# A diffusion layer on one Trainium2 core: sixteen modulation units move from the mixer into the first feed-forward block

## The reference

```python
m_x = split(silu(c) @ w_ada + b_ada, 9)          # 9 vectors of 1024
m_c = split(silu(c_ctx) @ w_ada + b_ada, 9)
x   = x   + 0.5 * m_x[2] * swiglu(modulate(rmsnorm(x, g0), m_x[0], m_x[1]), ffn1)
ctx = ctx + 0.5 * m_c[2] * swiglu(modulate(rmsnorm(ctx, g0), m_c[0], m_c[1]), ffn1)
px = modulate(rmsnorm(x, g1), m_x[3], m_x[4]) @ w_in
pc = modulate(rmsnorm(ctx, g1), m_c[3], m_c[4]) @ w_in
y  = concat(retention(px, pc), gmlp(px))
x  = x + m_x[5] * (y @ w_out)
x  = x + 0.5 * m_x[8] * swiglu(modulate(rmsnorm(x, g2), m_x[6], m_x[7]), ffn2)
return rmsnorm(x, final_g)
```

## Time and profile before

| what | value |
|---|---|
| timed runs, median (lowest to highest) | 2081.57 us (2080.06 to 2083.95) |
| the profiled execution, and its span | 2077.21 us, 2075.4 us |
| PE busy | 2018.5 us, 97% of the span |
| DVE, ACT, POOL busy | 1267.8, 753.2, 495.3 us |
| granted TensorE clock, mean over the span | 0.989 |
| chain of work that ended last | PE 85%, DVE 9%, ACT 3% |

### The profile page before, as it was taken

The page is one execution under the profiler, slowest core; times in us unless marked ns, Lnnn a source line. Parts: engine busy times, 40 slices in busy tenths (PEclk is TensorE's granted clock), DMA queues, the critical chain, the costliest instruction groups (busy, mean ns, idle before and its releaser), DMA issues.

```text
span 2075.4 us, 26060 instructions
## 1 busy us (share of the span) xinstructions
PE 2018.5 (97%) x10112; PEld 1690.5 (81%) x10112; DVE 1267.8 (61%) x1883; ACT 753.2 (36%) x1093; POOL 495.3 (24%) x311
## 2 busy tenths in 40 slices
PE   8999999999999999999999999898999999999997
PEld 4999978888888887887988898676788888888886
DVE  4987765556555466575353458889565555455555
ACT  3233533333333354463212222246333333344342
POOL 1000033323211102023323223455323322210002
PEclk9999999999999999999999999999999999999998
DMA  7874426656444776641010333421566644466664
GB/s 307 344 273 145 153 78 219 200 192 231 161 130 160 242 234 177 212 145 62 21 41 21 115 119 122 142 102 56 176 204 209 215 155 167 148 209 194 193 193 153
DMA packets 104042, 343.52 MB, mean 166 GB/s; under 512 B 11760, under 2 KB 13040, under 8 KB 86896
## 3 DMA queue, kind: packets, MB, share of 16 engines
q1 hardware_dynamic: 99312, 325.08, 46.3%
q10 hardware_dynamic: 4608, 16.78, 2.5%
HBM read 267.36 MB, written 74.45 MB: 165 GB/s over the span
## 4 chain that ended last, share of the span: by engine, by line
PE 85%; DVE 9%; ACT 3%; issue 2%; DMA 1%; POOL 1%; SPq 0%; ACTq 0%; DVEq 0%; POOLq 0%
PE PS L2111 13%; PE PS L2113 13%; PE PS L2112 12%; PE PS L1966 7%; PE PS L1968 6%; PE PS L1967 6%; PE PS L2151 6%; PE PS L2153 6%; PE PS L2152 6%; PE PS L2069 4%; DVE AS L1431 2%; PE PS L2024 1%; PE PS L2324 1%; DVE WVL L1551 1%; DVE DG L1323 1%
## 5 line engine op out<-in xcount | busy, mean ns | idle before, releaser
L2111 PE MATMUL PS<-HH,WVH 128*128 128x512 f32 x672 | 265.1, 395 | 0.0
L2113 PE MATMUL PS<-HH,WVL 128*128 128x512 f32 x672 | 263.7, 392 | 0.0
L2112 PE MATMUL PS<-HL,WVH 128*128 128x512 f32 x672 | 262.0, 390 | 0.0
L1966 PE MATMUL PS<-HH,WH 128*128 128x512 f32 x416 | 168.5, 405 | 3.2 <-DVE WL L1727 3.2
L1551 DVE TENSOR_TENSOR WVL<-WR,WVH 128x512 fp32r<-128x512 f32 x160 | 115.1, 719 | 88.2 <-ACT WVH L989 88.1
L1967 PE MATMUL PS<-HL,WH 128*128 128x512 f32 x416 | 164.4, 395 | 0.0
L1968 PE MATMUL PS<-HH,WL 128*128 128x512 f32 x416 | 164.3, 395 | 0.0
L1594 DVE TENSOR_TENSOR HL<-HLF,HH 128x1024 fp32r<-128x1024 f32 x76 | 104.8, 1386 | 80.5 <-ACT HH L1037 80.4
L2113 PEld LDWEIGHTS PS<-HH,WVL 128*128 128x128 f32 x672 | 126.1, 188 | 30.0
L2112 PEld LDWEIGHTS PS<-HL,WVH 128*128 128x128 f32 x672 | 126.1, 188 | 28.2
L2111 PEld LDWEIGHTS PS<-HH,WVH 128*128 128x128 f32 x672 | 126.4, 188 | 26.8
(11 more groups left out here) (262 smaller groups left out, 4843.1 us busy)
## 6 DMA issues: line engine op xcount, KB each, us to landing
WR<-w_units SPq DMA_DIRECT2D x89, 1024.0 KB, 5.8
gated<-HB SPq DMA_DIRECT2D x44, 512.0 KB, 6.7
down_weight_sums<-WB SPq DMA_DIRECT2D x22, 1024.0 KB, 3.9
gated_sums<-TBF SPq DMA_DIRECT2D x22, 768.0 KB, 4.2
AW<-w_units ACTq DMA_DIRECT2D x32, 512.0 KB, 4.3
HLF<-down_weight_sums SPq DMA_DIRECT2D x46, 256.0 KB, 3.3
AW<-ada_units SPq DMA_DIRECT2D x11, 1024.0 KB, 13.7
W2RB<-w_units SPq DMA_DIRECT2D x22, 512.0 KB, 3.6
```

The costliest lines, as they stand in the source:

```text
L1966: pe.matmul(dst, wh, xh, start=first, stop=False)
L2111: pe.matmul(bank[:, :], wh, xh, start=first, stop=False, skip_group_check=True)
L2112: pe.matmul(bank[:, :], wh, xl, start=False, stop=False, skip_group_check=True)
L2113: ins = pe.matmul(bank[:, :], wl, xh, start=False, stop=k == 3, skip_group_check=True)
```

## The change

Three things change.

- The latents' units leave the mixer. Units 20 to 27 are worked in the periods g = 14 to 21 of the first block: DVE sums the first half of a unit ahead of `up_first`, the second half behind it; PE makes the columns behind product 4. Units 28 to 35 are worked in the down product of the first block, half a unit behind `ring_low` of step 10, 13, 18, 21, 26, ... 69; PE makes their sixteen columns together behind step 72, and DVE adds their biases before the mixer's norm work begins. The loads are one DMA of 1 MB each on SyncE's queue; ACT issues none.
- In the openings of both blocks `gate_second(1, 1)` stands behind the first sum and the first low part of the next weights, no longer behind all of them.
- Two of the first eight units (6 and 7 in the order of loading) are split like the other operands: ACT makes the high part, DVE the low part, PE multiplies 16 times in fp32r instead of 8 times in float32, with a stationary of four columns for the high part. Product 5 goes ahead of `norm_scale` on PE. The first unit's load is one DMA and no longer two halves. The exponentials of the decay go from the start into the context's periods 2 and 3.

```diff
+ADA_SPLIT = (6, 7)
-ADA_SLOTS = ((10, 5), (11, 0), (11, 2), (12, 0), (12, 2), (13, 0), (13, 3), (14, 3), (14, 7), (15, 1), (15, 4), (15, 7),
-             (16, 1), (17, 1), (18, 1), (19, 1))
+ADA_PERIODS = {14 + i: ADA_CTX + i for i in range(8)}
+ADA_STEPS = tuple(range(ADA_CTX + 8, N_ADA))
 
...
+        AWL = {n: at(f"AWL{n}", [P, KT, UC], F32R, 65728 + 8192 * (n % 4)) for n in ADA_SPLIT}
+        CSS = at("CSS", [P, KT, 4], F32R, R + 40960)
+        SEL = at("SEL", [4, 2], F32, R + 41216)
...
+        def latent_places(a):
+
+            if a in ADA_STEPS:
+                i = a - ADA_STEPS[0]
+                return HLF[:, :, UC * (i % 2):UC * (i % 2 + 1)], HHF[:, i, 0:UC], PS[1]
+            return AWB[:, :, :], ASB[:, a % 2, :], PS[5]
...
-            for half in range(2):
-                k = slice(4 * half, 4 * half + 4)
-                sp.dma_start(AW[0][:, k, :], ada_units[0][:, k, :]).then_inc(s_half if half == 0 else s_first[0], 16)
+            ada(0)
...
+                def latent_unit(a):
+                    if a in ADA_STEPS[:2]:
+                        sp.wait_ge(s_m[1], NF)
+                    elif a in ADA_STEPS:
+                        sp.wait_ge(s_adv, sums_count(a - 2))
+                    elif a == ADA_CTX:
+                        sp.wait_ge(s_w2st, 16 * HALF)
+                    else:
+                        sp.wait_ge(s_adv, sums_count(a - 1))
+                    sp.dma_start(latent_places(a)[0], ada_source(a)).then_inc(s_first[a % 2], 16)
...
+                    if f == 0 and g + 1 in ADA_PERIODS:
+                        latent_unit(ADA_PERIODS[g + 1])
...
+                    if f == 0 and s % 8 == 6 and s // 8 < len(ADA_STEPS):
+                        latent_unit(ADA_STEPS[s // 8])
...
+            for n in ADA_SPLIT:
+                act.wait_ge(s_first[n], 16)
+                act.activation(split_high(n), AW[n][:, :, :], ACT.Copy).then_inc(s_awh, 1)
...
-            def latent_unit(u):
-
-                for half in range(2):
-                    k = slice(4 * half, 4 * half + 4)
-                    if u == ADA_CTX:
-                        act.wait_ge(s_fill, FILL["yscale", HEADS - 1, 1] + 1)
-                    else:
-                        act.wait_ge(s_adv, sums_count(u - 1) - 1 + half)
-                    act.dma_start(AW2[:, k, :], ada_source(u)[:, k, :]).then_inc(s_first[half], 16)
-
...
+            def split_low(n):
+
+                dve.wait_ge(s_awh, ADA_SPLIT.index(n) + 1)
+                dve.tensor_tensor(AWL[n][:, :, :], AW[n][:, :, :], split_high(n).bitcast(F32), ALU.subtract).then_inc(s_awl, 1)
...
-            def latent_sums(a):
+            def latent_sums(a, half):
 
 
                 sums, links = sums_count(a - 1), 15 * sums_count(ADA_CTX - 1) + 6 * (a - ADA_CTX)
-                acc = AS2[a % 2]
-                if a > ADA_CTX + 1:
-                    dve.wait_ge(s_col, a - 1)
-                for k in range(KT):
-                    if k % 4 == 0:
-                        dve.wait_ge(s_first[k // 4], 16 * (a - ADA_CTX + 4))
-                    w, c = AW2[:, k, :], CS[:, k, 0:1]
+                unit, acc, _ = latent_places(a)
+                if half == 0:
+                    dve.wait_ge(s_first[a % 2], latent_load_count(a))
+                    if a in ADA_STEPS:
+                        dve.wait_ge(BS[0].m[1], NF)
+                    elif a > ADA_CTX + 1:
+                        dve.wait_ge(s_col, a - 1)
+                for k in range(4 * half, 4 * half + 4):
+                    w, c = unit[:, k, :], CS[:, k, 0:1]
                     if k == 0:
-                        ins = dve.tensor_scalar(acc[:, :], w, c, None, ALU.mult)
+                        ins = dve.tensor_scalar(acc, w, c, None, ALU.mult)
                     else:
                         if k == 4:
                             dve.wait_ge(s_adv, sums + 1)
                         else:
                             dve.wait_ge(s_asum, links + k - k // 4)
-                        ins = dve.scalar_tensor_tensor(acc[:, :], w, c, acc[:, :], ALU.mult, ALU.add)
+                        ins = dve.scalar_tensor_tensor(acc, w, c, acc, ALU.mult, ALU.add)
                     ins.then_inc(s_adv if k % 4 == 3 else s_asum, 1)
 
             dve.wait_ge(s_const, 16 * 6)
                 dve.wait_ge(s_hi, b + 1)
...
-            dve.wait_ge(s_exp, 1)
-            dve.tensor_scalar(LG[:, :], LG[:, :], -1.0, None, ALU.mult).then_inc(s_lg, 1)
             ada_rows(4)
             ada_mods(2)
+            split_low(6)
+            ada_rows(5)
             dve.wait_ge(s_rb, J[0, 0] + 1)
-            for k in range(KT):
+            for k in range(4):
                 scaled(0, 0, k)
             ada_mods(3)
             first_gain(1)
-            ada_rows(5)
+            split_low(7)
+            for k in range(4, KT):
+                scaled(0, 0, k)
+            ada_rows(6)
             ada_mods(4)
-            ada_rows(6)
             ada_mods(5)
             first_gain(2)
             block_low(0)
...
-                def next_weights(g):
+                def next_weights(g, between=lambda n: None):
                     dve.wait_ge(s_wl, weights_done(f, g - 1, ORDER1[-1] if f and g == 2 else 6))
                     dve.wait_ge(s_wraw, 16 * g)
-                    weight_sums(g, lambda n: weight_low(g, n))
+                    def low_and_more(n):
+                        weight_low(g, n)
+                        between(n)
+                    weight_sums(g, low_and_more)
                     weight_low(g, 2)
                     weight_low(g, 3)
...
                 def block_period(g, q):
+                    a = ADA_PERIODS.get(g) if f == 0 else None
                     weight_low(g, 5)
                     gated(g - 1, 1 - q, 0)
+                    if a is not None:
+                        latent_sums(a, 0)
                     up_first(g, q)
+                    if a is not None:
+                        latent_sums(a, 1)
                     if g + 1 < NF:
                         next_weights(g + 1)
                     gate_second(g, q)
                         weight_low(g + 1, 4)
                     else:
                         ring_low(0)
+                    if a is not None:
+                        latent_mods(a)
                     up_second(g, q)
                     gated(g, q, 1)
                     if g + 1 < NF:
                     token_low(2, k)
                 up_first(1, 1)
...
                 up_first(1, 1)
                 dve.wait_ge(s_wl, weights_done(f, 1, 5))
-                next_weights(2)
-                gate_second(1, 1)
+                next_weights(2, lambda n: gate_second(1, 1) if n == 0 else None)
                 weight_low(2, 4)
                 up_second(1, 1)
...
                 if s % HALF == 3 and s > HALF:
                     down_added(0, s // HALF - 1)
+                if s >= 10 and (s - 10) // 8 < len(ADA_STEPS) and s % 8 in (2, 5):
+                    latent_sums(ADA_STEPS[(s - 10) // 8], s % 8 == 5)
                 if s == 22:
                     add_squares(1, 0)
...
+            dve.wait_ge(s_col, N_ADA)
+            for a in ADA_STEPS:
+                latent_mods(a)
...
+            def split_product(n):
+                r, i = ADA_PE.index(n), ADA_SPLIT.index(n)
+                pe.wait_ge(s_awh, i + 1)
+                pe.wait_ge(s_mods, ADA_PE[r - 4] + 1)
+                for k in range(KT):
+                    pe.matmul(PS[r % 4][0:4, 0:UC], CSS[:, k, :], split_high(n)[:, k, :], start=(k == 0), stop=False,
+                              skip_group_check=True)
+                pe.wait_ge(s_awl, i + 1)
+                for k in range(KT):
+                    ins = pe.matmul(PS[r % 4][0:2, 0:UC], CSS[:, k, 0:2], AWL[n][:, k, :], start=False, stop=(k == KT - 1),
+                                    skip_group_check=True)
                 ins.then_inc(s_ada, 1)
...
             first_columns(1)
             first_product(4)
             first_columns(2)
+            first_product(5)
             norm_scale(0, 0)
             pe.wait_ge(s_ms, J[0, 0] + 1)
             ctx_columns(3, 0)
-            first_product(5)
             first_columns(4)
-            first_product(6)
+            pe.wait_ge(s_cs, 4)
+            split_product(6)
             first_columns(5)
-            first_product(7)
+            split_product(7)
             first_columns(6)
             first_columns(7)
             pe.wait_ge(s_mods, 6)
...
                     pe.wait_ge(s_u2, g)
                     product(g, q, 4)
+                    if f == 0 and g in ADA_PERIODS:
+                        latent_columns(ADA_PERIODS[g])
                     pe.wait_ge(s_u3, g)
...
                 if s == STEPS - MAJOR - 1:
                     pe.wait_ge(BS[0].fyd, 24)
                     norm_sum(1, 1)
+                    for a in ADA_STEPS:
+                        latent_columns(a)
```

103 lines of the change are left out of this document (46 added, 57 removed).

## The result

| | before | after |
|---|---|---|
| timed runs, median (lowest to highest) | 2082.65 us (2080.06 to 2083.95) | 2052.77 us (2052.50 to 2054.90) |
| ratio, 95% interval | | 0.986 (0.9843 to 0.9877) |
| profiled execution, span | 2077.21 us, 2075.4 us | 2052.53 us, 2050.7 us |
| granted TensorE clock, mean | 0.989 | 0.991 |

The kernel is 29.9 us faster; 2052.5 us was predicted. (With the fourth timed run the median of before is 2082.65; from 2081.57, where the prediction started, the gain is 28.8 us.) One reservation belongs here: the profiled execution of before lay 5.4 us under its median and that of after on it, so the two traces differ by 24.7 us only. The working added up traces; against the trace alone it was 4.4 us too hopeful.

What follows compares the result with a forecast made beforehand. PE was taken as busy nearly throughout, so only its idle time and half clock could be won. −14.2 − 14.5 + 0 + 2.05 + 0 − 2.5 = −29.1 us from 2081.57 gave 2052.5 us, range 2048 to 2057.

Steps and rivals of the forecast that it cites:

- gate sum: Openings of both blocks: one DVE instruction moved up past six removes PE waits and half clocks, saving 14.2 us.
- first units: First modulation units: 2.27 us diagonal wait and likely 3.0 us half clock go, whole load costs 1.2; −2.5 us taken.
- So I see nothing late next: Openings: the next tile's other weight sums and low parts, moved back 0.7 and some 0.8 us, still reach PE in time.
- Latents in the mixer: Mixer: three PE waits (10.3 us) and two half clocks (4.2 us) go; 14.5 us saved, bounds 7 and 16.
- Latents in the periods: Eight periods of the first block, one unit each: 0 us, bounds nothing below zero and +6 us (0.75 each).
- Latents in the down product: First block's down product: eight more units, in halves behind steps, fit the slack; 0 us taken, bound +6.
- One place has no slack: step 33: Down product: half a unit ahead of the context's scaling makes PE's 0.42 us wait 2.5 us; +2.05, otherwise +4.5 or 0.
- PE's cost moves only: End of the first block's down product: sixteen column matmuls stand together on PE, their cost only moved; no time added.

## Why the prediction was right, and where only its sum was

| term | predicted | measured |
|---|---|---|
| gate sum | −14.2 | −9.9 |
| latents (mixer −14.5, periods 0, down product +2.05) | −12.45 | −15.8 |
| first units | −2.5 | −3.6 |
| sum | −29.1 | −29.3 (parts), −29.9 and −28.2 (whole) |

The total is met to a microsecond, the terms are not: 4.3 us too much in one and 4.5 too little in the other two cancelled. That the total came so close is luck. The miss of the gate sum is clear of the uncertainty of a difference, that of the latents (3.4 us) just so, that of the first units (1.1 us) is not.

**Gate sum.** The working of the two openings is right to 0.1 us in the waits. The step that failed is "So I see nothing late next". It looked at PE's demand for the weights behind the sum, and not at the queue behind that. With its wait gone DVE worked without a pause up to the low part that frees the raw weights, so the next load was issued at 1437.3, landed 6.1 us later, and in the second period the gate sum behind eight operations came 2.08 us late (0.59 in the first block). The wait had moved on by one period. The half clock behind the second new wait, in half of the executions, is part of the 4.3 us as well.

**Latents in the mixer.** The mechanism is right, the size low. In the run with the latents left there PE waits 9.2 us for AS and MODS and a further 1.63 us for ACC close by, with the granted clock at 0.5 behind that from 1364 to 1371 us (3.4 us lost), and these went as well. Aligned by PE's instructions that run and the changed one differ by 27.1 us from 935 us to the end of the mixer. Some 7 of these are the columns, and 2.9 lie ahead of 950 us, at a half clock behind the wait for WL that also stands in the run with more latent work and so is not the latents'. That leaves 17.2 us against the 14.5 predicted. I had counted only waits whose row names the removed work.

**Latents in the periods.** Zero, as predicted, and with more room than the argument gave. It let DVE wait out all three of POOL's sums (3.9 us) and put the gate sum at 595.9, a tenth of a us before PE; the hold was 2.8 us, the idle times ahead of the weight sums took up the rest, and the gate sum is 2.0 us early, against 1.8 before. The run with four more operations used 1.4 us of these and left 0.7. What the ledger of a trace hides: the columns' 3.5 us leave the mixer and enter the periods, which changes no sum but looks like a loss in this stretch.

**Latents in the down product.** The failed step is "One place has no slack: step 33". The scale three steps earlier had less: there PE had waited 2.56 us already, so everything gained ahead of it was at risk, and 5.3 us were lost there in the run with the latents in the mixer; no term of the prediction has them. That the low part of step 32 slipped in ahead of GpSimd's pass before was a matter of 0.25 us (774.44 and 774.69 us); in the run with the latents in the mixer it fell behind it and took 4.84. What sets the wait is that GpSimd's pass begins at once behind its root RS and so stands beside whatever VectorE does next, the diagonal or the low part ahead of it; the run with the pass behind the scaling showed it (0.82 us of wait, 6.9 us gained). The late mean of the changed kernel accounts for no more than those 0.82. Step 33 cost nothing, since the wait ahead shielded it; with the pass in the middle it cost 6.6.

**Columns at the end.** "PE's cost moves only" is wrong by the half clock that they bring on, 3.4 us in that execution and 1.7 in most.

**First units.** The gain is there, by another road than the one counted on. The DG wait went; the half clock stayed and came to lie partly on a wait. The cost set against it, 1.2 us for the whole first load, did not come: the first product began 0.73 us later (6.47 for 5.74) but what follows the first two products began 0.35 us sooner (15.03 for 15.38). The second context unit starts 4.9 us sooner (47.3 for 52.2), where 2 to 3 were foretold; of this 3.6 us are left in the time.

## What to carry to other kernels

When a wait on the critical engine goes, list not only what is late next in the same round but what its supplier can no longer do in advance, above all the issue of its next load, and look one round further. Where PE waits already, however briefly, assume that it will wait longer once it arrives sooner, unless all that it waits for moves up with it; and when a pass that blocks another engine's port is moved, move it behind the whole urgent chain, not behind one link of it. A prediction whose sum is right should be checked by undoing its terms one at a time.

## What the runs showed of the hardware

- A VectorE operation beside a GpSimd pass of two 128x2048 subtractions is held until one of these ends: 0.42 us became 4.73 (DG), 0.34 became 4.65 (HHF), 1.22 became 5.64 (DLOW). The price does not depend on the size of the operation held but on how much of GpSimd's instruction is still to run: a second low part that began later in the same pass took 3.01 us. So what counts is which operations begin inside the pass, and whether PE waits for them.
- Thirty-two matmul records of one column each took 4.52 us, with PEld busy for 5.36 of 5.40 us, and the granted clock fell to 0.5 in them, though PE was busy throughout. In all ten traces with such a row it fell there or within 0.5 us of its end. Dealt out over three steps the clock stayed at 1, in both traces.
- A wait of 1.19 us was not followed by a half clock at the scale, one of 1.21 for ACC was in some executions of the same kernel and not in others. Half clocks behind short waits move from run to run and are poor evidence for a microsecond or two.
